# Gates stage of a hybrid trunk: 0/1 tiles made token by token from a bf16 iota and an index column in SBUF

## The reference, cut to what matters

```python
q = (h @ w_q).reshape(bn, t, PEER_HEADS, 2, PEER_HALF)
s = einsum('bthcd,hckd->bthck', q, keys)
s_top, i_top = lax.top_k(s, PEER_TOPK)                     # 16 of 128 keys, twice per head
cand_s = s_top[..., 0, :, None] + s_top[..., 1, None, :]   # 16 x 16 sums per head
cand_i = i_top[..., 0, :, None] * PEER_NKEYS + i_top[..., 1, None, :]
best_s, pos = lax.top_k(cand_s, PEER_TOPK)
idx = take_along_axis(cand_i, pos, axis=-1)                # expert = row i * 128 + column j
gates = softmax(best_s, axis=-1)
...
pre = einsum('ced,cd->ce', take(u_tab, ii), hh)
act = gelu(pre)
out = einsum('ce,ced->cd', act * gg, take(v_tab, ii))
```

## Time and profile before

| | |
|---|---|
| median of 3 runs | 4153.09 us (4151.8 to 4156.67) |
| span of the profiled execution | 4139.5 us |
| its busy shares | TensorE 94%, VectorE 77%, ScalarE 47%, GpSimd 28% |
| gates stage of layer 0 | about 594 to 1470 us from the span's start |
| gates stage of layer 1 | about 2935 to 3540 us |

### The profile page before, as it was taken

How to read it: one execution, slowest core, us unless ns; L and a number is a source line. 1 busy time by engine, 2 the same in 40 slices (tenths; PEclk the granted TensorE clock), 3 DMA queues, 4 the chain that set the end, 5 groups by cost and what they waited for, 6 DMA issues and landing times. The chain is left out here.

```text
span 4139.5 us, 63328 instructions
## 1 busy us (share of the span) xinstructions
PE 3881.7 (94%) x20946; PEld 3333.0 (81%) x20946; DVE 3194.6 (77%) x5918; ACT 1963.3 (47%) x3786; POOL 1169.6 (28%) x905
## 2 busy tenths in 40 slices
PE   8998988999999989999997999778899999899998
PEld 2787877788888868888886777657899999899997
DVE  2698789999997768888886555658998877677777
ACT  2212234777777722222223555433488887333333
POOL 0232212343443334444442222123122222122221
PEclk9999999999999999999999999979999999999999
DMA  7443116899999999999991111022589898899996
GB/s 295 163 162 113 46 54 216 305 326 334 331 341 339 334 358 372 375 373 377 373 373 60 55 46 46 31 77 66 183 299 308 308 309 312 306 333 332 333 332 219
DMA packets 411884, 1026.09 MB, mean 248 GB/s; under 512 B 33968, under 2 KB 182448, under 8 KB 405680
## 3 DMA queue, kind: packets, MB, share of 16 engines
q1 hardware_dynamic: 296496, 604.22, 41.5%
q0 software_dynamic: 110592, 402.70, 26.8%
q10 hardware_dynamic: 4608, 16.78, 1.1%
HBM read 904.03 MB, written 119.54 MB: 247 GB/s over the span
## 5 line engine op out<-in xcount | busy, mean ns | idle before, releaser
L136 ACT ACTIVATE w_hi<-w_raw 128x1024 fp32r<-128x1024 f32 x536 | 568.3, 1060 | 1174.1 <-PE psum L1428 881.9
L168 PE MATMUL psum<-h_hi,w_hi 128*128 128x512 f32 (+1 forms) x2208 | 853.0, 386 | 89.6 <-PEq L809 32.8
L170 PE MATMUL psum<-h_hi,w_lo 128*128 128x512 f32 (+1 forms) x2208 | 832.5, 377 | 0.0
L169 PE MATMUL psum<-h_lo,w_hi 128*128 128x512 f32 (+1 forms) x2208 | 832.3, 377 | 0.0
L147 DVE TENSOR_TENSOR w_lo<-w_raw,w_hi 128x1024 fp32r<-128x1024 f32 x424 | 519.4, 1225 | 387.2 <-ACT w_hi L136 366.7
L1426 PE MATMUL psum<-a_hie,w_hi 128*128 128x512 f32 (+1 forms) x2048 | 756.6, 369 | 31.0 <-DVE a_loe L1499 31.0
L1428 PE MATMUL psum<-a_hie,w_lo 128*128 128x512 f32 (+1 forms) x2048 | 756.7, 369 | 0.0
L1427 PE MATMUL psum<-a_loe,w_hi 128*128 128x512 f32 (+1 forms) x2048 | 754.1, 368 | 0.0
L1298 POOL DMA_INDIRECT u_rowsg<-in_peer_u_rows,expert_idx x384 | 446.1, 1162 | 1050.9 <-DVE u_rowsg L1053 919.4
L1407 POOL DMA_INDIRECT v_rowse<-in_peer_v,expert_idx x384 | 421.1, 1097 | 830.1 <-DVE row_sume L1508 816.9
L1228 ACT ACTIVATE ojg<-eq_jg,gate_Tg 128x128 fp32r<-128x128 bf16 x1792 | 550.2, 388 | 109.9 <-DVE eq_jg L1076 109.4
(11 more groups left out here) (263 smaller groups left out, 5474.5 us busy)
## 6 DMA issues: line engine op xcount, KB each, us to landing
w_raw<-in_peer_u SPq DMA_DIRECT2D x256, 512.0 KB, 6.0
w_raw<-in_peer_v SPq DMA_DIRECT2D x256, 512.0 KB, 5.4
gates<-stageg SPq DMA_DIRECT2D x28, 2048.0 KB, 15.9
acts<-act_gg SPq DMA_DIRECT2D x128, 256.0 KB, 5.1
gte<-gates SPq DMA_DIRECT2D x32, 1024.0 KB, 8.3
act_fe<-acts SPq DMA_DIRECT2D x128, 256.0 KB, 6.0
ada_w<-in_ada_w SPq DMA_DIRECT2D x12, 2048.0 KB, 8.7
ada_rows<-in_ada_w SPq DMA_DIRECT2D x48, 512.0 KB, 3.8
```

What stands on the lines that cost most here:

```text
L136: act.activation(self.weights(s)[0], self.raw[:, slot, :], ACT.Copy).then_inc(self.hi_done, 1)
L168: pe.matmul(out, wh, hi[:, k], start=(k == 0), stop=False)
L169: pe.matmul(out, wh, lo[:, k], start=False, stop=False)
L170: last = pe.matmul(out, wl, hi[:, k], start=False, stop=(k == KC - 1))
```

## The change

A group's two VectorE instructions over four tokens, which compare a repeated f32 iota with four columns of indices read from PSUM and repeated along the keys, become eight instructions over one token each, which compare a bf16 iota with one index per partition, held in SBUF (`place_T`). For that the indices of a block are first copied from PSUM to SBUF, once a block, with a wait for the 0/1 tiles of the block before. The tile `half_u` loses its own memory: the shift by four is now done in place on `pos`, so that it comes after the bit mask and is waited for alone. The values computed are the same.

```diff
-        self.iota = sb("iota", [P, P])
+        self.iota = sb("iota", [P, P], BF16)
...
-        half_u = [sb("half_u", [P, HEADS, K], U32)[:], ex[:].bitcast(U32)]
+        half_u = [pos[:], ex[:].bitcast(U32)]
...
+        place_T = sb("place_T", [P, 2, P])
...
+                    if b:
+                        dve.wait_ge(oh_ready, b * GB)
+                    dve.tensor_copy(place_T[:].rearrange("p c x -> p (c x)"), t.psum[:, 6 + b % 2, 0:2 * P])
                     step(dve.tensor_copy(gate_T[:, b % 2].rearrange("p c x -> p (c x)"),
...
-                        x = t.psum[:, 6 + b % 2, c * P + r:c * P + r + 4]
-                        last = dve.tensor_tensor(eq[:, g % EQ], bc(t.iota[:].unsqueeze(1), [P, 4, P]),
-                                                 bc(x.unsqueeze(2), [P, 4, P]), ALU.is_equal)
+                        for j in range(4):
+                            last = dve.tensor_scalar(eq[:, g % EQ, j], t.iota[:], place_T[:, c, r + j:r + j + 1],
+                                                     None, ALU.is_equal)
...
-                    dve.tensor_single_scalar(half_u[0], pos[:], 4, ALU.logical_shift_right)
                     step(dve.tensor_single_scalar(half_u[1], pos[:], 15, ALU.bitwise_and))
+                    step(dve.tensor_single_scalar(half_u[0], pos[:], 4, ALU.logical_shift_right))
```

## The result

The median went from 4151.44 us (9 runs) to 4164.11 us (9 runs). The ratio is 1.0034, 95% interval 1.0024 to 1.0044: slower by 10 to 18 us, more than the 0.2% that can be told. The forecast was 4164.7, 11.6 us more than the 4153.1 that three runs of before had given; 12.7 us lie between the medians.

A forecast was written before the change was run, and what follows sets the result against it. VectorE was taken to set the pace from 712 us, be nearly balanced from 838, and have cover later. 45 groups x 0.23 us, plus 0.7 for the copy and 0.5 for the shift, made 11.6 on 4153.1: 4164.7 us, range 4143 to 4182.

The forecast's parts named there:

- VectorE sets the pace from 712 us, 20 groups in full: Gates stage, 712 to 838 us: VectorE nearly always busy, so added time counts in all 20 groups; 131 us instead of 126.
- A group 1.38 us by its instructions: Eight comparisons a group on VectorE: four at 0.19 and four at 0.155 us, 0.18 more than the 1.20 before.
- 0.05 us a group from meeting gathers: Comparison bursts on VectorE meet GpSimd gathers with chance about 0.45, at 0.12 us a meeting.
- Gathers longer than 0.94 us: Sign expected in the profile after: GpSimd gathers lasting beyond 0.94 us, beside some burst instructions at about 0.4 us.
- 12 of 28 groups in the balanced window, 2.8 us: From 838 to 1000 us, VectorE and TensorE nearly balanced: 12 of 28 groups count, bounds 7 and 28.
- 9 groups in the third window, 2 us: From 1000 to 1470 us: VectorE's free time covers the loss except in 9 stalled chains, one group each.
- Layer 1, two groups, 0.5 us: Layer 1's gates stage: 105 us free on VectorE over 94 groups covers all but 2; same length within 1 us.
- Copy of the indices and the shift, 1.2 us: Side effects on VectorE where it sets the pace: 0.7 us for the index copy, 0.5 for the selection's in-place shift.
- A: Rival: index operand costs nothing in a row, or bf16 is cheaper; a group 0.80 to 0.90 us, end 4141; chance 0.17.
- B: Rival: no difference, a group between -0.1 and +0.13 us, loss within 7 us, end 4156; chance 0.16.
- C: Rival: VectorE waits out the rest of each gather a burst meets, 0.48 us more a group, end 4183; chance 0.12.
- D: Rival: no fast mode with this operand or types, 0.88 us more a group, end 4222; chance 0.05.

The follow-up runs named there:

- the constants: The change with a constant per instruction in place of the index per partition (wrong experts, only times used), against the kernel before: 4137.67 us, ratio 0.9982.
- the dose: What a group takes longer on VectorE than in the kernel before, median over groups: 0.24 us for the change, 0.43 with four idle instructions (4178.50 us).
- the idle instruction: Kernel before with its old comparisons plus one unread two-input VectorE instruction a group, no index copy, bf16 iota and shift kept: 4157.03 us, ratio 1.0025.

## Why the prediction was right, point by point

- *VectorE sets the pace from 712 us, 20 groups in full:* shown. 131 us had been forecast for what took 126; measured from group to group it is 135.9 for 130.8.
- *A group 1.38 us by its instructions:* 1.44. The `eq_i` distance was 0.20 for 0.19, and `eq_j` 0.16 for the 0.155 taken in the middle of its bounds. The index operand costs 0.06 us where 0.05 had been read from the earlier trace rows. That its cost is not hidden behind the neighbour was the step that decided the sign, argued from the earlier trace rows; the constants show it directly. Here the formula on the Trainium skill's page "VectorE: DVE Perf Modes" (errata table: a fixed part plus elements over the mode's factor) gives by estimate 0.88 us a group; the run with constants took 0.95, and with the operand it is 0.56 too low. The factor of four for bf16 in its tier table agrees: an `eq_j` takes 0.035 us less than an `eq_i` (0.65 and 0.79 for four), about half of the 0.07 that 128 elements cost at 0.53 ns each.
- *0.05 us a group from meeting gathers:* wrong, it is nothing. 162 of the 224 groups overlap a gather; from the first start to the last end they take 1.521 us in the median, the other 62 take 1.520. The sign that the prediction had named did appear: 158 instructions that meet a gather last 0.32 to 0.45 us instead of 0.25 or 0.28. But the next ones start on time, 0.16 or 0.20 us after them as ever, so nothing is lost. The CAST of the earlier trace rows lasts longer in the same way, but there VectorE waits for the result before it goes on (its next instruction starts 0.03 us after its end), so that its 0.23 us count. This term and the 0.06 too little in the comparisons cancel, 0.23 against 0.24, which is luck.
- *Gathers longer than 0.94 us:* they are not so by the comparisons. The 104 gathers that begin while `eq_i` is made take 0.94 us in the mean. Those that begin while VectorE makes a `low` (L147, both inputs in SBUF) take 1.67, before and after, and of these there were 89 before and 104 after; hence the mean of 1190 ns instead of 1162. One of them:

```profile
723.70 1.22 DVE L147 TENSOR_TENSOR w_log<-w_raw,w_hig 128x1024 fp32r<-128x1024 f32 x1
```

```profile
724.05 1.68 POOL L1302 DMA_INDIRECT u_rowsg<-in_peer_u_rows,expert_idx  x1 [2.95 <-DVE u_rowsg L1054]
```

- *Two groups before 712 us, 0.5 us:* not to be read. The first matmul of group 2 starts between 712.7 and 715.1 us in all traces, in no order of the dose.
- *12 of 28 groups in the balanced window, 2.8 us:* the traces with 0.24 in layer 0 took 167.1 to 170.5 us, those without 165.1 to 167.4, 2.7 us more in the mean. Right in size, but with scatter as large.
- *9 groups in the third window, 2 us:* neither shown nor refuted; the means differ by 2.2 us (455.0 with the dose in layer 0, 452.8 without), but the scatter there is 10.
- *Layer 1, two groups, 0.5 us:* too small. The change in layer 1 alone costs 3 to 10 us. The profile after had been said to show the same length of layer 1 within 1 us; the two traces of the change are 10 and 4 us longer there. The free 105 us of VectorE had been read as cover for all groups. But in the trace before 97.7 of them are waits for ScalarE's `hi` in front of a `low` (3004 to 3540 us):

```profile
DVE w_lo L147 <- ACT w_hi L136: 78.5, 52, 5.3
DVE w_log L147 <- ACT w_hig L136: 19.2, 20, 2.0
```

  The order on VectorE is fixed, so such a wait cannot be used for the 0/1 tiles behind it. That this is why the cover fails is argued, not shown. In the trace of the change the lateness shows as TensorE's wait for `oj` in layer 1, 8.7 us in 9 groups from 3004 to 3560 us, where before it was 0.7 us in 2. How much of that is the dose and how much a transfer that came late is open: the profiled execution of the layer-1 run shows 1.2 us in 4 groups.
- *Copy of the indices and the shift, 1.2 us:* with all of it and the old comparisons the ratio is 1.0000 (0.9991 to 1.0009), which allows it and also nothing.
- *The sum:* 11.6 us forecast, 12.7 between the medians. Its base was not understood rightly: 13.6 us do not lie around the span, 1.8 do. Since the difference was added to the median of the runs, this did not matter. That 4164.7 meets 4164.11 so closely is partly luck: the three runs behind 4153.1 lie 1.7 us above the median of nine, the term of layer 1 was some 3 us too small (0.5 against the 4.0 between the means of the traces), and no run shows the 1.2 us of copy and shift. The bounds beside the forecast were also added up too narrowly: taken together they give 4156 to 4180, not 4157 to 4176.

Of the rivals, A (a cheap operand) is what the run with constants was: 12 us of gain by A's working, 4 to 11 measured. B would have needed a group at most 0.13 us longer; it is 0.24. C (quarrel over ports) is out by the idle instruction and by the met groups. The page "SBUF — State Buffer" of the Trainium skill (section on who interferes with whom) has the first to start hold the ports for its whole instruction; in the trace the comparisons run beside a gather of 0.94 us unhindered, and the gathers that begin among them are not longer. D did not come: the distances are 0.20 and 0.16 us, not 0.26.

## What to carry to other kernels

Before a wide instruction is cut into narrow ones in a faster mode, compare distances from start to start, not durations, and count the fixed part of every one with its per-partition operand: here 0.20 us for 128 elements of which 0.07 were elements. Here the faster mode was better had in the wide instruction, by a layout whose innermost step is one for all operands (0.34 us for 512 elements). An engine's free time in a window need not be cover: look at what the engine waits for in it, and in front of which work, before calling a stretch covered.

## What the runs showed of the hardware beyond that

- An index per partition costs a `tensor_scalar` of 128 elements 0.06 us, back to back as well (0.95 against 1.44 us for eight).
- VectorE in its fast modes and a GpSimd gather at the same time: no delay of the burst (1.44 us with and without), and none of the gather (0.94 us where it begins during an `eq_i`). A gather that begins during `low`, one instruction of 1.22 us with two inputs in SBUF, takes 1.67 us in the mean.
- A two-input comparison with all operands bf16 and an innermost run of only two elements took 0.34 us for 512 elements against 0.60 for the form with an input in PSUM; the 0.26 saved is 512 times half of the 1.04 ns that an element costs there. One operand was repeated over the keys by a step of zero further out.
